# Start-up, first projection and expert routing of a two-layer decoder step put in another order

## The reference, cut to what matters

```python
(q, kc, vc, ks, vs, kw, vw, g_nsa, u, o_pre, if_pre, g_a, g_b) = split_cols(h @ prm['w_in'])
q = q.reshape(b, t, NSA_KV_HEADS, NSA_GROUP, HEAD_DIM) * (HEAD_DIM ** -0.5)
...
bias = jnp.moveaxis(rel_bias(table, dist).reshape(nq, nc, NSA_KV_HEADS, NSA_GROUP), 1, 3)
...
xp = xp + channel_mixer(rmsnorm(xp, norm_ffn[l]), l, ...)   # layer 0 dense, layer 1 experts
...
logits = (x @ router).astype(jnp.float32)
top_val, top_idx = lax.top_k(logits, TOP_K)        # 2 of 8 experts
gate = jax.nn.softmax(top_val, axis=-1).reshape(-1)
...                                                # rows sorted by expert, blocks of 128 rows
yd = lax.map(lambda a: swiglu(a[0], w1[a[1]], w3[a[1]], w2[a[1]]), (xd.reshape(n_blocks, MOE_BLOCK, d), blk_e))
```

## Time and profile before

| | us |
|---|---|
| three runs, median (lowest to highest) | 1739.11 (1737.37 to 1745.32) |
| the profiled execution, device time | 1742.53 |
| its span | 1740.9 |
| PE busy | 1673.4 (96%) |
| DVE busy | 1097.4 (63%) |
| ACT busy | 841.1 (48%) |
| POOL busy | 176.7 (10%) |
| DMA | 424.95 MB, mean 244 GB/s |

### The profile page before, as it was taken

How to read it: one execution, slowest core, us unless ns; L and a number is a source line. 1 busy time by engine, 2 the same in 40 slices (tenths; PEclk the granted TensorE clock), 3 DMA queues, 4 the chain that set the end, 5 groups by cost and what they waited for, 6 DMA issues and landing times.

```text
span 1740.9 us, 23573 instructions
## 1 busy us (share of the span) xinstructions
PE 1673.4 (96%) x8772; PEld 1379.4 (79%) x8772; DVE 1097.4 (63%) x1289; ACT 841.1 (48%) x900; POOL 176.7 (10%) x237
## 2 busy tenths in 40 slices
PE   7999999999999999999998999999999999999996
PEld 4877677699999897777765788888888888888884
DVE  1563524465654364541534688888888888888897
ACT  2343422044443233431203577676777777777764
POOL 1421013100000433002210100000000000000030
PEclk9999999999999999997996999999999999999999
DMA  9549242645543864333182899999999999999993
GB/s 249 163 161 289 79 121 73 183 140 158 181 158 109 211 205 145 98 96 85 38 285 85 329 329 399 358 391 367 382 395 362 399 349 398 352 402 346 399 388 105
DMA packets 232202, 424.95 MB, mean 244 GB/s; under 512 B 34462, under 2 KB 129982, under 8 KB 231932
## 3 DMA queue, kind: packets, MB, share of 16 engines
q1 hardware_dynamic: 219292, 383.62, 63.3%
q0 software_dynamic: 12832, 40.28, 7.3%
HBM read 403.70 MB, written 24.29 MB: 246 GB/s over the span
## 4 chain that ended last, share of the span: by engine, by line
PE 88%; DVE 5%; ACT 2%; DMA 2%; issue 1%; DVEq 1%; SPq 0%; ACTq 0%
PE ps L762 84%; PE ps L766 4%; DVE weights_low L1830 2%; ACT weights_high L1426 2%; DMA weights_in<-in_moe_w 1%; DVE arena L1830 1%; DVEq L2051 1%; ACT arena L1426 0%; DVE arena L2052 0%; DMA arena<-in_vecs 0%; DVEq L2446 0%; DVE arena L2554 0%; DVE arena L1979 0%; ACT arena L1423 0%; DVE arena L2350 0%
## 5 line engine op out<-in xcount | busy, mean ns | idle before, releaser
L1830 DVE TENSOR_TENSOR weights_low<-weights_in,weights_high 128x3072 fp32r<-128x3072 f32 (+1 forms) x192 | 589.4, 3090 | 107.3 <-ACT weights_high L1426 107.1
L1426 ACT ACTIVATE weights_high<-weights_in 128x3072 fp32r<-128x3072 f32 (+1 forms) x192 | 489.6, 2560 | 199.3 <-PE ps L762 170.3
L762 PE MATMUL ps<-arena 128*128 128x288 f32 (+16 forms) x2732 | 549.2, 370 | 32.8 <-DMA arena<-in_vecs 9.0
L762 PEld LDWEIGHTS ps<-arena 128*128 128x128 f32 (+7 forms) x2732 | 403.0, 182 | 164.6 <-issue 56.9
L762 PE MATMUL ps<-weights_high,item_high 128*128 128x512 f32 x704 | 279.4, 397 | 7.3 <-DVE weights_low L1830 6.7
L762 PE MATMUL ps<-weights_high,item_low 128*128 128x512 f32 x704 | 276.0, 392 | 0.0
L762 PE MATMUL ps<-weights_low,item_high 128*128 128x512 f32 x704 | 275.9, 392 | 0.0
L762 PEld LDWEIGHTS ps<-weights_high,item_high 128*128 128x128 f32 x704 | 133.4, 189 | 36.3 <-DVE weights_low L1830 9.0
L762 PEld LDWEIGHTS ps<-weights_high,item_low 128*128 128x128 f32 x704 | 133.2, 189 | 28.2
L762 PEld LDWEIGHTS ps<-weights_low,item_high 128*128 128x128 f32 x704 | 133.4, 189 | 26.7
L762 PE MATMUL ps<-weights_high,gated_high 128*128 128x512 f32 x352 | 139.0, 395 | 4.0 <-DVE gated_low L1830 3.4
(11 more groups left out here) (205 smaller groups left out, 1871.2 us busy)
## 6 DMA issues: line engine op xcount, KB each, us to landing
weights_in<-in_moe_w SPq DMA_DIRECT2D x192, 768.0 KB, 8.4
weights_in<-in_moe_w SPq DMA_DIRECT2D x48, 1536.0 KB, 9.8
weights_in<-in_moe_w SPq DMA_DIRECT2D x64, 512.0 KB, 5.1
ffn_in<-in_ffn_w SPq DMA_DIRECT2D x30, 1024.0 KB, 7.2
weights_in<-in_moe_w SPq DMA_DIRECT2D x16, 1024.0 KB, 9.4
arena<-in_w_in SPq DMA_DIRECT2D x32, 384.0 KB, 4.1
arena<-in_w_in SPq DMA_DIRECT2D x32, 256.0 KB, 4.9
token_slots<-arena SPq DMA_DIRECT2D x12, 512.0 KB, 7.5
```

The costliest lines, as they stand in the source:

```text
L762: return nc.tensor.matmul(out, lhsT, rhs, start=start, stop=stop)
L1426: return nc.scalar.activation(out, x, ACT.Copy, scale=scale)
L1830: return V.tensor_tensor(out, x, y, op)
```

## The change

The constants are put in another order and split in four loads. PE starts with seven products of a tile `R` of zeros that nothing reads. The input rows' transposes and the query projection's first group come before all bias products. The query weights arrive from the host with the two key groups' heads already side by side, so three loads replace eight, for both layers; they are issued before the rest of the constants and the router. The shifted reads (`Lh`, and a four-fold `Ls` for the sample group) are issued after the key/value weights, and the bias products stand between the blocks of the key/value projection, with eight products of 60 columns in the place of two of 120, and three products over 32 rows in the place of twelve over 8. ACT evicts the prompt biases, DVE the others. The gate bias goes to POOL's queue. In routing `by_tokens` follows one step behind instead of two; `h2` is made of rows times gain in two halves of columns, the first before the logits; the division by the norm goes into `Sel0` (`selr`), and POOL multiplies `h2` by it later, ahead of the scatter. The gathered block is evicted in two halves. PE gets six, and later three, products whose result nothing reads (`awake`) where it waits. `AHEAD` is 6.

```diff
@@ sync
+            sp.dma_start(cst[:, 0:P], a["const"][:, 0:P]).then_inc(s_xin.sem, 16)
...
+            sp.dma_start(cset[0:NBUCKET, :], a["const"][0:NBUCKET, NKEEP:NSET]).then_inc(s_tab.sem, 16)
...
-                        put(s, [(dst[:, :, g, v, :], src[:, :, g, v, :]) for g in range(G) for v in range(KVH)])
+                        put(s, split(pslot(s, KD, n), w[:, :, 0:n], (0, 3, 6, 8)))
...
             mixer_chunk(0, 0)
+            sp.dma_start(cst[:, P:NKEEP], a["const"][:, P:NKEEP]).then_inc(s_setup.sem, 16)
+            sp.dma_start(router[:, :, :], a["router"][0].rearrange("(k p) e -> p k e", p=P)).then_inc(s_setup.sem, 16)
+            sp.wait_ge(w8_ev.sem, w8_ev.at(0))
+            sp.dma_start(scr, w8[0:H, :]).then_inc(w8_st.sem, 16)
             mixer_chunk(0, 1)
...
             mixer_chunk(0, 2)
+            for h in range(H):
...
+                sp.dma_start(Lh[h // 4][:, h % 4, :], src).then_inc(hank.sem, 16)
@@ tensor
+            pe.wait_ge(warm_ev.sem, warm_ev.at(0))
+            for i in range(7):
+                mm(ps[:, 0, 0:N], R[:, 0:P], R)
...
+                    if g == 1 and l == 0:
+                        pe.wait_ge(s_setup.sem, s_setup.at(0))
+                        pe.wait_ge(w8_ev.sem, w8_ev.at(0))
...
+                        if l == 0 and i == 0:
+                            pe.wait_ge(hank.sem, hank.at(0))
+                            pe.wait_ge(cb_in.sem, cb_in.at(0))
+                            pe.wait_ge(q_ev.sem, q_ev.at(0))
+                        if l == 0 and i < 2:
+                            prompt_bias(2 * i)
+                            prompt_bias(2 * i + 1)
+                        elif l == 0 and i == 2:
+                            other_biases()
...
-                    elif d >= 2:
-                        by_tokens(d - 2)
+                    elif d >= 1 and l == 1:
+                        by_tokens(d - 1)
...
+                    awake(6)
                     pe.wait_ge(xt2_ev.sem, xt2_ev.at(0))
                     pe.wait_ge(sel_d.sem, sel_d.at(0))
...
+                    awake(3)
                     pe.wait_ge(x0_d.sem, x0_d.at(0))
...
-                    i.then_inc(x_pe.sem, 1)
+                        if k % 4 == 3:
+                            i.then_inc(x_pe.sem, 1)
@@ vector
+                    if l == 1 and d == 7:
+                        dve.wait_ge(wf_in.sem, wf_in.at(0))
+                        rows_weighted_ffn(0)
...
+                    tt(selr, sel[:, :, 0], rsd, ALU.mult)
+                    rows_weighted_ffn(1)
@@ gpsimd
+            pool.wait_ge(x_pe.sem, 2)
+            for m in range(3):
...
+                nc.gpsimd.tensor_tensor(h2[0:n, m, :], h2[0:n, m, :], bass.AP(x.tensor, x.offset, [x.ap[0], [0, D]]), ALU.mult)
```

More of the change, by code:

```diff
@@ L117, in constants @@
     put("future", np.tile(np.where(dist < 0, NEG, 0.0), (H, 1)))
+    set_cols = sum(p.shape[1] for p in parts)
+    put("rev", np.eye(P)[::-1])
+    put("rowsel", np.tile(np.eye(NS), (1, P // NS)))
     own = np.zeros((P, 2, NS))
@@ L137 @@
 NB_U = len(BODY)
-AHEAD = 2
+AHEAD = 6
 def landed(units, u):
@@ L396, in build @@
         nbB = rtake(P)
-        gmx, gsum, fss, frs, rsd = (rtake(3) for _ in range(5))
+        gmx, gsum, fss, frs, rsd, selr = (rtake(3) for _ in range(6))
         fsq = rtake(6).rearrange("p (m i) -> p m i", m=3)
@@ L530, in loaded @@
         def loaded(s, u, l):
[L532 removed]
+            return 48 * (u + 1)
         FIRST = (3, 2, 2)
@@ L733, in _ @@
                     sp.dma_start(gfin, bass.AP(gf.tensor, gf.offset, [[0, P], [1, D]])).then_inc(gf_in.sem, 16)
+                    for u in range(2, AHEAD):
+                        kind, ch, j = BODY[u]
+                        sp.wait_ge(used.sem, u + 7)
+                        unit(0, kind, ch, j, (LEAD + u) % NRAW)
                     sp.wait_ge(items.sem, items.at(0))
@@ L1298, in _, with awake @@
                 else:
-                    by_tokens(KD - 2)
+                    def awake(n):
+                        for i in range(n):
+                            mm(ps[:, 1, 0:N], ident, xT[:, i, :])
                     by_tokens(KD - 1)
@@ L1468, in _ @@
                     dense_rounded(l, i)
+                    if l == 0 and i < 4:
+                        for j in (2 * i - 4, 2 * i - 3):
+                            act.wait_ge(bias_pe.sem, bias_pe.at(0, j + 1))
+                            copy(biasP[:, 2 * j:2 * j + 2, :].rearrange("p h x -> p (h x)"), ps[:, 2 + j % 2, :]
+                                 ).then_inc(bias_ev.sem, 1)
                 act.wait_ge(kv_ev.sem, kv_ev.at(l))
@@ L1790, in _ @@
                     fn(gx[:, :, :], gx[:, :, :], ACT.Exp).then_inc(lgx_a.sem, 1)
-                    item_high(0)
+                    for b in range(2):
+                        act.wait_ge(x_pe.sem, b + 1)
+                        copy(Xh[:, 4 * b:4 * b + 4, :].rearrange("p k s -> p (k s)"), ps[:, 4 + b, :]).then_inc(x_h.sem, 1)
                     high_first(3)
@@ L1911, in _ @@
                     dense_rest(l, 2 + 2 * f)
+                    if l == 0 and f == 1:
+                        other_biases()
                     for m in range(3):
```

210 lines of the change are left out of this document (102 added, 108 removed).

## The result

Five executions of the changed kernel took 1708.0, 1719.0, 1719.8, 1720.1 and 1720.2 us (median 1719.8), five of the kernel before 1737.4 to 1745.3 (median 1739.1). The ratio is 0.9875, with a 95% interval of 0.9847 to 0.9903: faster by 19 us. Four more executions in the study (run 1) lie at 1708.1 to 1718.6, so over nine the median is 1718.6. Two of the nine lie at 1708, one at 1712.9 and six at 1717.8 to 1720.2, and the mean granted clock of each follows: 0.990 and 0.989 for the three, 0.983 to 0.985 for the six. The profile that is read here is one of the two at 1708: it took 1708.0 us, its span is 1706.4, while the profile of before stood at 1742.5 and 1740.9. Its 34.5 us are therefore more than the kernel gains as a rule, and have to be taken apart.

A forecast was written before the change was run, and what follows sets the result against it. PE was taken as the bound, busy 96% of the span, with waits and half clock at the start and in routing. Gains of 11.6 and 13.6 us, 25.2 together, from the 1739.1 median gave 1714 us (chance 0.50), range 1703 to 1729.

The forecast's parts named there:

- Start, forecast 17.1 - 5.5 = 11.6: Kernel start: norm earlier by 17.1 us, less 5.5 for bias products coming later; net 11.6 us, bounds 6.2 and 17.2.
- The norm's gain: Start: the norm, at 42.9 us before, moves to 25.8; gain 17.1 us, bounds 14.2 and 21.7.
- Its weights land by 13 us: Start, query projection's group 0: its 2 MB of weights behind the input rows land by 13 us, ahead of need.
- The bias products: Inside the key/value projection: 3.4 us of 512-column instructions and 2.1 of short ones, together 5.5 us, bounds 4.5 and 8.
- The reads of the shifted table: Key/value projection: the shifted reads land at 30 to 34 us, while PE asks for them near 44 us.
- Routing, forecast 13.6: Routing to first expert products: 10.7 us up to the first expert product and 2.9 in the products behind; sum 13.6.
- The gather went from 15.07 to 8.52: Routing: the gather's 15.07 us at half clock become 7.6 at full clock, gain 7.5 us.
- GpSimd's products: Routing: POOL's three products of h2, 5.8 us behind the gather and ahead of the scatter, cost 0.
- The clock falling in routing anyway: Rival: the clock falls in routing in spite of the fillers; price 11.2 us, time 1725 us, chance 0.20.
- Clock held at the start: Rival: the clock holds from the zeros to the norm; 4.6 us more gain, time 1709 us, chance 0.12.
- Data the bound: Rival, start: weights and constants come late; gain 4 us less, 1718, or 1723 with waits for `hank`; chance 0.11.
- need not recur: Layer 1: a 20 us half-clock stretch in the profiled execution before, costing 7 us on one group, need not recur.

The follow-up runs named there:

- run 1: The changed kernel again, unchanged: 1718.6, 1712.9, 1708.1 and 1717.8 us, ratio to the kernel before 0.984.
- run 2: The changed kernel without the 18 filler instructions of TensorE in routing: median 1726.7 us.
- run 3: The kernel before with only the start's edits, routing as before: 1728.1 us, ratio 0.992.
- run 7: The changed kernel with GpSimd's three products of h2 behind the wait for the slots instead of ahead of it: one execution, 1702.5 us.
- run 6: The changed kernel with three more products of zeros behind the table's products at the start: median 1717.3 us.
- run 4: The kernel before with only routing's edits, the start as before: 1727.0 us, ratio 0.993.
- run 12: The kernel before with only fillers added in routing, six and seven products in two waits: median 1732.0 us, ratio 0.9951.
- run 5: The changed kernel with gate tile 12 moved between the turning of the sample probabilities and their values, both layers: median 1727.3 us over ten.
- run 8: The changed kernel with the bias products inside the key/value projection made twice: one execution, 1726.3 us.
- run 9: The changed kernel with three filler products ahead of each wait for turned sample probabilities: 1712.1, 1713.4, 1714.6 us; a fourth of 2387 us left out.
- run 11: The changed kernel without the seven products of zeros at the start: median 1720.1 us.
- run 10: The changed kernel with the edits of run 6, run 7 and run 9, and five filler products ahead of the third compressed tile's turning: median 1710.9 us.

## Why the forecast of 1714 us was right, and where it was not

The measured gain is 19.3 us by medians, 23.4 on the chip of run 1, the forecast's 25.2. The range of 1703 to 1729 held it, and the likeliest case is the one that came: clock kept in routing, lost and regained at the start. Its own band of 1710 to 1718 was missed by a little, with 1719.8 and 1718.6 over nine.

**Start, forecast 17.1 - 5.5 = 11.6.** The norm's gain was forecast as 17.1 and is 17.7 in this profile, 17.8, 16.0 and 17.2 in those of runs 1, 2 and 3. Part of that is luck, since two steps of it were wrong and nearly cancel: the input rows landed at 9.63, not at 8.0, but PE was through with zeros and table at 7.87, not at 9.5, and rested, so that the transposes began within 0.2 us of the forecast. They took 6.38 with the two of the vectors, as put (5.7 and 0.7); group 0 and the norm's products ended 9.3 us after them, not 9.9. "Its weights land by 13 us" was a step that failed outright: PE waits for them until 14.8 in run 7 and 16.1 in run 6, which bounds the rival that would hold the clock from zeros to norm. It exists (run 7's norm is at 22.9) but is worth 1 to 2.5 us, not 4.6. The bias products were put at 5.5 and cost 5.3 when doubled. The reads of the shifted table were to land at 30 to 34 us and did so at 42.0 in run 7, the one profile with a wait for them, from PE's timeline:

```profile
42.05 1.98 PE L767 MATMUL ps<-arena 128*128 128x512 f32 x4 [0.55 <-DMA arena<-bias_scratch]
```

In the first profile PE asks for them at 43.8. If they landed there as in run 7, the slack was some 2 us where the forecast had 10, and the overlap came true by little. At the sample values of layer 0 the start's net gain is 12.6 in the first profile, 9.6 in run 1 (231.89 - 222.34) and 11.9 in run 3; by medians the start alone gave 10.7. All of these lean on one profile of before, and that one was quick at the start: runs 4 and 12 have the same start, but there the clock fell for 6.8 us at 35 us, the query projection took 22.6 us (run 12) where before took 19.6, and the sample values stand at 236.06 and 235.74 instead of 231.89. Against these the start gains up to 4 us more.

**Routing, forecast 13.6.** Point by point in the first profile: the gather's start gained 22.8 - 20.9 = 1.9, as forecast. The gather went from 15.07 to 8.52, a gain of 6.6 and not 7.5; this term was mis-sized. It was halved with the clock, but its products alternate between 128 and 32 rows, and of every six starts the four at and just behind such a turn lie 0.35 to 0.37 us apart at half clock and 0.20 to 0.21 at full, so 0.57 of the time is left. The earlier trace rows had nearly that ratio (8.77 / 15.96 = 0.55), and the forecast quoted it without using it. The copies off the chain gave 1.3, as forecast: 2.35 us between gather and expert product before (955.38 - 953.03), 1.04 now (924.73 - 923.69). The first expert product is 30.65 - 20.9 = 9.8 us nearer, forecast 10.7. Of the products behind it 2.0 us came, forecast 2.9, and the missing 0.8 is PE's new wait for DVE beside GpSimd's products. The last 1.9 us of the 13.6 are no part of the change: 1.6 of them stand in the last item, where the clock fell once in the trace of before and not in this one. The routing part in the seven other profiles with the same routing (runs 1, 4, 5, 6, 8, 9, 11) is 867.3 to 868.5, 11 to 12 us below before's 879.5, and routing alone gave 11.8 by medians. So 13.6 should have been 11.7.

**Costs put at nothing.** GpSimd's products were not free: "5.8 us ahead of the scatter" looked at who waits for them, not at who works beside them. In the first profile they hold up DVE for 3.2 us (1.90 and 1.74 where 0.19 and 0.22 stood) and PE for 0.8. The Trainium skill, SBUF — State Buffer, section "SBUF: two separate sides", has it that VectorE and GpSimd share one pair of ports: between a GpSimd operation and a VectorE operation with two SBUF inputs or in a two-port mode, whichever starts first holds the pair for its whole instruction while the other waits. The rows of run 7 agree: each slow operation of DVE is about as long as one product of GpSimd. The prediction had weighed only that GpSimd is the slower engine for such work, and there the row says 1.5 times (5.65 / 3 = 1.88 us, VectorE's 1.28 in the trace of before) rather than twice. The list's six units and the gate biases did not appear in any wait.

**Rivals.** The clock falling in routing anyway (0.20): not seen across the gather in any of the eleven profiles that have fillers there, runs 4 and 12 among them; without them it fell in all three. Its price was put at 11.2 us and is 9.4 by the traces (11.5 - 2.1), 8 to 11 by the times of run 2; what would be left was put at 2.4 and is 2.1. Clock held at the start (0.12): it came in run 7, for less; in runs 6, 7 and 10 the clock stood at 1.00 through all 26 transposes, so transposes do not always end at half clock, as one rule that the prediction weighed would have it. Data the bound (0.11): it was right about the query weights once the clock holds, and half right about `hank` (42 us, but a wait of 0.5 us and not 5). The chances of the four cases that are faster add up to 0.93, where 0.94 was put.

**The 5 us between 1714 and 1718.6.** Two come from routing (11.7 for 13.6) and one from the start (10.7 for 11.6); the rest is less than the medians tell. The level of 1714 itself leans on what the forecast set aside as what "need not recur": the half-clock stretch in layer 1 of before. It recurs. Eleven profiles have the wait of 1.1 us ahead of the sample values in both layers (before, the first, runs 1, 2, 3, 4, 6, 7, 8, 11, 12): the long fall stands in seven of them, once in each, in layer 0 (runs 1, 2, 3, 6, 11) or layer 1 (before, run 8), and in four not at all. What makes it one pass and not the other stays open.

The profiles put the price of the fall at 8 to 11 us: from the transposes ahead of it in layer 0 to those in layer 1, 551.4 in run 1 against 543.2 in run 7, and in layer 1 85.1 us in before against 74.3 in the first profile (861.41 - 776.31, 840.50 - 766.19). One such fall takes 0.006 from the mean granted clock, which is the distance between the changed kernel's executions at 1708 and at 1719. Time and granted clock go together in before too (1730 at 0.985 to 1748 at 0.974), without levels. Whether the new start makes the fall more frequent was not shown: by profiles it is seven of nine against one of three (counting run 5's at its new place), but of run 4's eight executions, with the old start, four have 0.985 to 0.987 where its profiled one, without a fall, has 0.991.

## What to carry to other kernels

In this kernel a wait of 1.1 us on TensorE was worth little by itself and could cost ten: look, in more than one profile, for the same instructions at two durations, and fill the wait in front of them before moving any work. When a term is scaled by the clock, take the ratio from a row at both levels instead of two. An elementwise product given to GpSimd was paid for by VectorE's small operations beside it, so look for a place where VectorE is idle; `item_low`, which reads PSUM, took 0.69 us beside such a product (924.35) and without one (920.13). And before a difference is read off one profile, look at how far the profiles of unchanged parts lie apart: 4 us at the start here.

## What the runs showed of the hardware that was not expected

- The clock fell behind a wait of 1.1 us (run 1, at 223 us) and stayed at 0.50 for 17 us although PE was busy all the while (12.00 of 12.00 us, 41 instructions); in the first profile, with the same wait, it did not. Runs 2, 3, 6 and 11 show the same fall with 20.5 us, and run 8 in layer 1. With the wait filled (runs 9 and 10) no profile has it.
- The clock fell over the row transposes when PE had rested 1.1 to 1.8 us ahead of them (first profile, runs 1, 2, 3, 5, 8, 9), and did not after a rest of 0.97 us (run 7) or none (runs 6, 10).
- Turns between 32-row and 128-row products did not halve with the clock: 0.35 us at 0.50, 0.20 to 0.21 at 1.00 (0.213 and 0.112 between products of 128 rows); the whole gather has a ratio of 0.57.
- Beside one fp32 product of GpSimd on 128 x 1024, a DVE operation of 0.19 us takes 1.90, and four of GpSimd's six scatters take 3.2 to 4.1 us where they overlap DVE's splitting of weights, where in the trace of before, with no splitting beside them, none took over 1.1.
